# Moving six modulation pairs of a two-block transformer kernel from TensorE to GpSimd, and cutting one gate slot of the even attention in two

## The reference

```python
def first_block(x, c, ada_w, ada_b, norm_g, ...):
    cs = jax.nn.silu(c)
    for layer in range(DEPTH):                       # 2 layers: even, odd
        mod = cs @ ada_w[layer] + ada_b[layer]       # (1, 1024) @ (1024, 3072)
        shift, scale, gate = jnp.split(mod, 3, axis=-1)
        h = rms_norm(x, norm_g[layer]) * (1.0 + scale[:, None, :]) + shift[:, None, :]
        y = even_mixer(h, ...) if layer % 2 == 0 else odd_mixer(h, ...)
        x = x + gate[:, None, :] * y
    return rms_norm(x, final_g)
```

## Time and profile before

| | us |
|---|---|
| median of three runs | 1269.30 (1268.88 to 1269.52) |
| the profiled execution | 1269.58 |
| its span, first to last instruction | 1267.80 |
| granted TensorE clock, mean | 0.998 of full speed |

### The profile page before, as it was taken

How to read it: one execution, slowest core, us unless ns; L and a number is a source line. 1 busy time by engine, 2 the same in 40 slices (tenths; PEclk the granted TensorE clock), 3 DMA queues, 4 the chain that set the end, 5 groups by cost and what they waited for, 6 DMA issues and landing times.

```text
span 1267.8 us, 24526 instructions
## 1 busy us (share of the span) xinstructions
PE 1243.5 (98%) x10376; PEld 1124.6 (89%) x10376; DVE 827.1 (65%) x1237; ACT 684.4 (54%) x887; POOL 99.0 (8%) x83
## 2 busy tenths in 40 slices
PE   6999999999999999999999999999999999999997
PEld 5998899879999999999888888999999999888886
DVE  3667856886866969766655545766978766655443
ACT  2556446765856567245544435856567345544433
POOL 0000000000000430230000000000330230000000
PEclk9999999999999999999999999999999999999999
DMA  9867665724434433235455554444433225555452
GB/s 385 300 257 275 258 233 186 258 98 165 169 133 166 167 133 134 69 104 194 167 198 172 195 192 172 169 133 167 167 133 117 86 100 192 190 173 193 166 193 73
DMA packets 35101, 222.91 MB, mean 176 GB/s; under 512 B 3888, under 2 KB 8240, under 8 KB 9264
## 3 DMA queue, kind: packets, MB, share of 16 engines
q1 hardware_dynamic: 31248, 216.23, 48.4%
q10 hardware_dynamic: 3744, 5.11, 1.2%
HBM read 220.28 MB, written 1.05 MB: 175 GB/s over the span
## 4 chain that ended last, share of the span: by engine, by line
PE 92%; DVE 3%; ACT 2%; DMA 2%; issue 1%; SPq 0%; ACTq 0%; POOL 0%; DVEq 0%
PE pj L637 62%; PE yv L637 14%; PE sc L637 10%; PE tp L637 4%; DVE ring_rounded L751 1%; PE tp L503 1%; DMA ring<-weights 1%; PE tp L2005 1%; DMA xT<-x_t 1%; DVE att_area L580 1%; ACT att_area L534 0%; ACT w_split L742 0%; ACT probsT L1671 0%; DVE att_area L605 0%; DVE big L1878 0%
## 5 line engine op out<-in xcount | busy, mean ns | idle before, releaser
L751 DVE TENSOR_TENSOR ring_rounded<-ring,w_split 128x2048 fp32r<-128x2048 f32 x106 | 248.2, 2347 | 60.1 <-ACT w_split L742 58.0
L2231 DVE TENSOR_TENSOR ring_rounded<-ring,big_rounded 128x2048 fp32r<-128x2048 f32 x66 | 151.3, 2293 | 107.2 <-ACT big_rounded L2102 107.1
L742 ACT CAST w_split<-ring 128x2048 fp32r<-128x2048 f32 x106 | 202.2, 1908 | 31.7 <-PE pj L637 22.6
L637 PE MATMUL pj<-h_split,w_split 128*128 128x256 f32 x1264 | 172.3, 286 | 0.2 <-ACT w_split L2489 0.2
L637 PE MATMUL pj<-h_split,ring_rounded 128*128 128x256 f32 x1264 | 165.5, 281 | 1.3 <-DVE ring_rounded L751 1.3
L637 PEld LDWEIGHTS pj<-h_split,w_split 128*128 128x128 f32 x1264 | 156.4, 189 | 6.5 <-issue 5.3
L637 PEld LDWEIGHTS pj<-h_split,ring_rounded 128*128 128x128 f32 x1264 | 155.9, 188 | 2.8 <-DVE ring_rounded L751 2.1
L2102 ACT CAST big_rounded<-ring 128x2048 fp32r<-128x2048 f32 x66 | 126.2, 1912 | 50.1 <-PE pj L637 40.6
L637 PE MATMUL pj<-hT_rounded,w_split 128*128 128x256 f32 x1136 | 146.2, 280 | 0.0
L637 PEld LDWEIGHTS pj<-hT_rounded,w_split 128*128 128x128 f32 x1136 | 139.4, 189 | 0.0
L637 PE MATMUL sc<-big_rounded 128*128 128x512 f32 x176 | 68.8, 391 | 0.0
(11 more groups left out here) (379 smaller groups left out, 2128.2 us busy)
## 6 DMA issues: line engine op xcount, KB each, us to landing
ring<-weights SPq DMA_DIRECT2D x180, 1024.0 KB, 4.8
big<-weights SPq DMA_DIRECT2D x20, 1024.0 KB, 7.6
first_block<-biases ACTq DMA_DIRECT2D x26, 192.0 KB, 4.7
first_block<-biases SPq DMA_DIRECT2D x6, 192.0 KB, 10.6
xT<-x_t SPq DMA_DIRECT2D x1, 1024.0 KB, 9.3
out_t<-scr SPq DMA_DIRECT2D x4, 256.0 KB, 2.9
con<-constants SPq DMA_DIRECT2D x1, 897.0 KB, 6.8
aux<-small SPq DMA_DIRECT2D x1, 832.0 KB, 10.3
```

The source lines that it names most:

```text
L637: return nc.tensor.matmul(out, lhsT, rhs, start=start, stop=stop, skip_group_check=True)
L742: act.post(nc.scalar.copy(w_split[:, w % 2], ring[:, in_ring(idx)]), s["w_high"])
L751: dve.post(nc.vector.tensor_tensor(ring_r[:, at], ring[:, at], w_split[:, w % 2].bitcast(F32), ALU.subtract), s["w_low"])
L2231: dve.tell(nc.vector.tensor_tensor(w_low(t, i), w, value(w_high(i)), ALU.subtract), s["ffn_low"])
```

## The change

Twelve modulation slots (six pairs: gate of the even layer, shift and scale of the odd one) leave TensorE's list of slots and become six entries `mod0_4` to `mod1_3`. GpSimd multiplies each slot in place by the eight values of silu(c) for each partition (four `tensor_scalar` of 128x512 for a slot), adds the parts (three `tensor_tensor` for the first slot of a pair, four for the second) into two rows of the tile `raw`, and signals `mod_read` after each slot. TensorE then sums over partitions with four products against one column of ones, and DVE copies four columns.

The entries stand in steps 1, 3, 5 and 7, behind the last step, and (`mod1_3`) between `even_out1` and `even_out2`. Steps 0, 2 and 8 lose their pair. SP issues the twelve loads at places given by `MOD_AFTER`, into the same three buffers, each behind a wait for its buffer. `dve_mod(1)` moves into the loop over `even_out`. `even14` (the third gate slot) is run in two halves of its inner dimension: the first half in the fill of step 7, the second at the start of step 8. A semaphore of the second block is merged into another.

The core of the diff:

```diff
-    "even": {-1: ["even5"], 0: ["even6", "ada0_8", "ada0_9"], 1: ["even8"], 2: ["even13", "ada0_10", "ada0_11"],
-             3: ["even7", "ada1_4", "ada1_5"], 4: ["even9"], 5: ["even10", "ada1_6", "ada1_7"], 6: ["even11"], 7: ["even14"],
-             8: ["ada1_0", "ada1_1"], 9: ["even15"], EVEN_TAIL: ["ada1_2", "ada1_3"]},
+    "even": {-1: ["even5"], 0: ["even6"], 1: ["even8", "mod0_4"], 2: ["even13"], 3: ["even7", "mod0_5"], 4: ["even9"],
+             5: ["even10", "mod1_0"], 6: ["even11"], 7: ["mod1_1", "even14"], 9: ["even15"], EVEN_TAIL: ["mod1_2"]},
+MOD_AFTER = (3, 4, 5, 9, 11, 12, 13, 14, 15, 16, 17, 18)
-EARLY_BY = 6
+EARLY_BY = 5
...
+                for j in mods_behind.get(i, ()):
+                    if j < OWN:
+                        before, _ = head_use[mod_buffer(j)]
+                        sp.wait_ge(slot_done, before + 1)
+                    else:
+                        sp.wait_ge(s["mod_read"].sem, j - OWN + 1)
+                    sp.dma_start(mod_weights(j), mod_d[j]).then_inc(landed[mod_buffer(j)], 16)
...
+        def pe_mod(pe, name):
+            n = MODS.index(name)
+            use = bank_use(name)
+            pe.eng.wait_ge(bank_free[use % NPJ], use // NPJ)
+            pe.eng.wait_ge(s["mod_read"].sem, 2 * n + 2)
+            for m in range(4):
+                last = matmul(bank_of(name)[:, m:m + 1], mod_sum(n)[:, m // 2, (m % 2) * P:(m % 2 + 1) * P],
+                              C("ones")[:, 0:1], m == 0)
+            last.then_inc(slot_done, 1)
+        def pool_mods(pool):
+            pool.eng.wait_ge(s["cond_ready"].sem, 1)
+            for n, name in enumerate(MODS):
+                ...
+                for half in range(2):
+                    ...
+                    for k in range(4):
+                        ins = nc.gpsimd.tensor_scalar(w[k], w[k], cs[:, 4 * half + k:4 * half + k + 1], None, ALU.mult)
+                    pool.do(ins)
+                    ...
+                    for k in range(1, len(terms)):
+                        ins = nc.gpsimd.tensor_tensor(total, terms[0] if k == 1 else total, terms[k], ALU.add)
+                        if k < len(terms) - 1:
+                            pool.do(ins)
+                    pool.tell(ins, s["mod_read"])
...
+            def pe_even_half(k):
+                if k == EVEN_TAIL - 2:
+                    pe_split(pe, EVEN_HALVED, ks=range(KC // 2, KC))
+            pe_attention(pe, "even", pe_even_half)
...
             for i in range(KC // 2):
+                if i == 2:
+                    pe_mod(pe, MOD_LAST)
...
-            dve_mod(dve, 1)
             for i in range(KC // 2):
+                if i == 2:
+                    dve_mod_columns(dve, MOD_LAST)
+                    dve_mod(dve, 1)
                 dve_residual(dve, "even_out", lambda ch: mod[:, 16 + ch:17 + ch], (i,))
                 dve_lows(dve, min(IDX[f"even_out{i}"] + 2, IDX["even_out3"]))
```

## The result

The changed kernel takes **1299.87 us** (median of 4 runs, 1299.32 to 1301.49) against 1269.09 of the kernel before in the same comparison: a ratio of 1.0242, interval 1.023 to 1.0254, **30.8 us slower**. I had forecast 1276.5 and a range of 1265.6 to 1288. The direction is right, the size is not, and the mechanism that made most of it is my third rival, which had a chance of 0.12 and a price of 7 to 10 us on top of the forecast's own wait.

A forecast was written before the change was run, and what follows sets the result against it. TensorE, busy for 98% of the span, was taken as the bound. Terms -9.4 + 4.5 + 0.4 + 0.6 + 0.3 = -3.6 us, plus 10.8 for DVE's waits, made +7.2 on 1269.3: 1276.5 us, range 1265.6 to 1288.

The forecast's parts named there:

- my third rival: Even attention: GpSimd becomes the bound and TensorE waits for `mod_read`, 7 to 10 us at `mod1_3`, 1285 us; chance 0.12.
- the forecast's own wait: Even attention, steps 0 to 7: DVE instructions wait for GpSimd beyond DVE's room, costing TensorE 10.8 us.
- the price of the scaling: GpSimd's one-input scaling of 128x512: 0.75 us assumed, between a cast at 0.37 and an addition at 1.28.
- The meeting with DVE: Even attention: GpSimd and 44 DVE instructions (low parts, normalising, L516) exclude each other at shared ports; the later one waits.
- its mean wait: Mean wait w of one such DVE instruction for GpSimd in the even attention: 0.5 us; 0.4 and more had chance 0.44.
- My own table: Time by mean DVE wait: 0.3 us over at w = 0.1, 4.1 at 0.3, 10.8 at 0.5, some 21 at 0.75.
- the rooms of steps 5 and 7: DVE's spare time before TensorE must wait, in steps 5 and 7 of the even attention: 0.9 and 0.6 us.
- the halves: `even14` in two halves: its first low product comes earlier than DVE has room for; 0.3 us, between 0 and 0.6.
- The sum of -3.6: Net change in us before GpSimd and DVE disturb each other: five pairs leave TensorE, products and small stalls come.
- Four one-column products: TensorE's added products for each of six modulation entries: 0.75 us for four, 4.5 us in all.
- The two bank waits: TensorE waits for reused banks behind `even15` and in `even_out`: 0.4 and 0.6 us.
- The deadlines: Three slots done ahead of the attention, nine (68 us) within 95 us up to `mod1_3`: GpSimd stays ahead of TensorE.

The follow-up runs named there:

- the run without arithmetic: The changed kernel with GpSimd's scalings and additions replaced by clearing one column per slot, the products reading zeros: 1268.91 us, ratio 0.999.
- five executions of nine: The changed kernel with GpSimd working but nobody waiting for it before the odd attention, later loads left out: median 1274.36 us; these five 1272.7 to 1274.4.
- the run with the whole slot and no arithmetic: The changed kernel without GpSimd's arithmetic and with `even14` in one piece again: 1268.44 us, ratio 0.999.

## Why the prediction failed

**The step that failed is the price of the scaling.** "I take 0.75, a little under the middle, since it has one input like the cast", with 1.28, the addition, as the upper bound. Measured: 1.56 undisturbed, and 1.95 in the mean, outside the bounds. I had bounded it by the number of inputs, from a cast of a quarter of its size and another operation. No row of before showed that a second input makes an instruction longer on GpSimd. Eight of them make a pair 20.7 us instead of 15, and with what DVE takes 26: the last sum came at 200.2 us, where the run without arithmetic wants it at 170.8. By the Trainium skill (GPSIMD Engine Reference, Performance versus the Vector engine) a tight loop over 512 elements takes 769 ns at best; the rows of this instruction say 1.56 us, and the measurement decides.

**Rival three had the mechanism, with too small a price.** I put it at 7 to 10 us, at `mod1_3` alone. Two slots were done ahead of the attention, at 70.9 us, not the three that I counted. The other ten took until 200.2: some 104 us of their own and 21 beside DVE, where I had 27 for nine, so that part was of the right size. But I gave the case a chance by asking whether the price would be at its upper bound, and the bound was too low. Nor did I price what comes behind such a wait: of the loss 7.8 us are slots that run longer, mostly at a lower clock.

**The meeting with DVE was right in kind, and its mean wait too large.** The kinds of instructions are those that I listed: L622 waits 0.42 in the mean, L619 0.30, L784 0.15. For the 44 instructions that makes 24 x 0.416 + 8 x 0.303 + 8 x 0.15 = 13.6, with 0.5 for L533 14.1 us, a mean of 0.32 where I took 0.5. My own table gives 4.1 us for 0.3; measured were 3.8 to 5.5 in five executions of nine and about 11 in the others, of which there is no trace. By the rule that the forecast states, the rooms of steps 5 and 7 are 1.3 and 1.4 us, not 0.9 and 0.6 (0.75 of step 7 it had spent on the halves already); the 10.8 at 0.5 are then 9.4. By what I wrote would show it, the low parts missed (2.44 us, not 2.6 to 2.8), L622 met it (0.770, not under 0.7), and TensorE's 5 to 15 us of waits for DVE were 2.3.

**The sum of -3.6 was nearly right as far as the odd attention.** In the run with the whole slot and no arithmetic the first scores there start at 206.95 instead of 210.00, 3.05 earlier.

```profile
206.95 1.13 PE L670 MATMUL sc<-big 64*128 64x256 f32 x8
```

Four one-column products take 0.87, not 0.75, which alone makes 0.7 in six. The two bank waits came as 0.44 to 0.47 and 0.43 (0.4 and 0.6 forecast), and `even14` to the last values stayed at 3.91 in the change. But in the median of the runs only 0.5 to 0.9 us arrive. Part goes where the clock falls behind step 8, 1.5 us in the profile of the run without arithmetic, and part in the second block, where in the same profile TensorE stands still for 1.0 us near 990 us with no releaser shown; before, it did not; no load or product of the change stands there, and the cause is open.

**The deadlines** were right: at 0.92 for a scaling, no wait for GpSimd is left, and the time is the forecast one. That the terms then add up to it is luck: by the medians the gain is 0.5 instead of 3.6, and the meeting at that price 1276.43 - 1268.91 = 7.5 instead of 10.8. Both are about 3 us too large, with opposite signs.

## What to carry to other kernels

Before work goes to an idle engine, price its instruction by a row of the same operation and form, or leave the upper bound open. A case in which the new engine becomes the bound decides over the sign, so its chance hangs on that one price. Give such an engine only what it can finish well ahead of the first use, and look at what its waits put in front of others in a shared queue: three pairs instead of six were faster than both kernels only once the loads behind a wait had been put ahead of it.

## What the runs showed of the hardware

- On GpSimd a scaling of 128x512 by a scalar takes longer (1.56 us from a column, 1.49 by a constant) than a multiplication of two tensors (1.04) or an addition (1.18). From 512 to 2048 columns the multiplication goes from 1.04 to 3.60, 1.67 ns a column.
- A DVE low part that meets GpSimd can stand still for nearly all of a GpSimd instruction, 3.04 us against one of 3.60. By the Trainium skill (SBUF — State Buffer, Who interferes with whom) the shared port pair is under an exclusive lock; the rows agree, and these show its length. GpSimd pays as well: its scalings by a scalar lose 0.39 us in the mean, those of two tensors 0.24, but beside these its additions lose more (mean 1.63 against 1.47), so that it loses some 30 us in all with either. DVE loses less with the first form than with the second (0.42 and 0.74 at L622). Why was not tried, and the form alone is not shown to be the cause: with scalings by a scalar of half the width L622 loses 0.51.
- TensorE's clock fell towards 0.5 behind waits of 1.0 and 0.8 us in one run and to 0.62 behind one of 2.44 in another, and stayed at 1.00 behind one of 2.45 in a third (one execution each).
